# The last norm of a two-layer encoder: two of eight tiles multiplied on GpSimd, one square root for two columns, one projection block moved ahead of attention values

## The reference, cut to what matters

```python
def rms_norm(x, g):
    xf = x.astype(jnp.float32)
    y = xf * lax.rsqrt(jnp.mean(xf * xf, axis=-1, keepdims=True) + EPS)
    return (y * g.astype(jnp.float32)).astype(x.dtype)

def reference(x, ...):
    for i in range(2):
        h = rms_norm(x, mix_norm[i])
        x = x + (neighbourhood_attention(h, ...) if i == 0 else sliding_window_gqa(h, ...))
        x = x + squared_relu_mlp(rms_norm(x, mlp_norm[i]), ...)
    return rms_norm(x, final_norm)
```

## Time and profile before

| | |
|---|---|
| time, median of 3 runs (lowest, highest) | 1142.25 us (1141.94, 1142.47) |
| the profiled execution's own time | 1142.17 us |
| its span, first to last instruction | 1140.5 us |
| PE busy | 1128.4 us, 99% of the span |
| DVE, ACT, POOL busy | 633.2, 512.3, 134.6 us |
| HBM read, written | 103.84 MB, 2.67 MB |

### The profile page before, as it was taken

How to read it: one execution, slowest core, us unless ns; L and a number is a source line. 1 busy time by engine, 2 the same in 40 slices (tenths; PEclk the granted TensorE clock), 3 DMA queues, 4 the chain that set the end, 5 groups by cost and what they waited for, 6 DMA issues and landing times.

```text
span 1140.5 us, 16574 instructions
## 1 busy us (share of the span) xinstructions
PE 1128.4 (99%) x5580; PEld 943.0 (83%) x5580; DVE 633.2 (56%) x1030; ACT 512.3 (45%) x922; POOL 134.6 (12%) x243
## 2 busy tenths in 40 slices
PE   8999999999999999999999999999999999999997
PEld 6888888888888888888888888888888888888886
DVE  7787887764442234444346888866443223444334
ACT  6777777553431124333235676644443122333221
POOL 6543341330000000000001222100000000000000
PEclk9999999999999999999999999999999999999999
DMA  6222231343222322232322112122223222332222
GB/s 227 94 91 91 93 91 55 98 120 105 92 92 97 106 92 92 94 108 77 108 92 93 45 59 60 52 93 93 92 92 102 101 92 92 99 103 93 92 92 93
DMA packets 34290, 106.97 MB, mean 94 GB/s; under 512 B 5760, under 2 KB 8096, under 8 KB 34256
## 3 DMA queue, kind: packets, MB, share of 16 engines
q1 hardware_dynamic: 29344, 98.61, 25.7%
q0 software_dynamic: 4768, 7.90, 2.9%
q10 hardware_dynamic: 144, 0.02, 0.0%
HBM read 103.84 MB, written 2.67 MB: 93 GB/s over the span
## 4 chain that ended last, share of the span: by engine, by line
PE 98%; DVE 0%; DMA 0%; ACT 0%; SPq 0%; issue 0%; DVEq 0%; ACTq 0%
PE acc L427 28%; PE acc L429 28%; PE acc L428 28%; PE om_ps L565 2%; PE pt_ps L741 2%; PE om_ps L589 1%; PE om_ps L561 1%; PE s_ps L531 1%; PE pt_ps L552 1%; PE s_ps L730 1%; PE s_ps L729 1%; PE om_ps L521 1%; PE s_ps L427 1%; PE s_ps L429 1%; PE s_ps L428 1%; DMA w_raw<-in_wstream 0%
## 5 line engine op out<-in xcount | busy, mean ns | idle before, releaser
L839 ACT CAST w_hi<-w_raw 128x1024 fp32r<-128x1024 f32 x179 | 187.9, 1050 | 387.8 <-PE acc L429 382.8
L427 PE MATMUL acc<-h_hi,w_hi 128*128 128x512 f32 x792 | 315.5, 398 | 1.7 <-DVE w_lo L1140 0.9
L429 PE MATMUL acc<-h_hi,w_lo 128*128 128x512 f32 x792 | 309.1, 390 | 0.0
L428 PE MATMUL acc<-h_lo,w_hi 128*128 128x512 f32 x792 | 308.8, 390 | 0.0
L1140 DVE TENSOR_TENSOR w_lo<-w_raw,w_hi 128x1024 fp32r<-128x1024 f32 x177 | 216.6, 1224 | 143.6 <-ACT w_hi L839 143.6
L427 PE MATMUL acc<-u_hi,w_hi 128*128 128x512 f32 (+1 forms) x624 | 240.6, 386 | 0.0
L429 PE MATMUL acc<-u_hi,w_lo 128*128 128x512 f32 (+1 forms) x624 | 239.5, 384 | 0.0
L428 PE MATMUL acc<-u_lo,w_hi 128*128 128x512 f32 (+1 forms) x624 | 239.5, 384 | 0.0
L427 PEld LDWEIGHTS acc<-h_hi,w_hi 128*128 128x128 f32 x792 | 148.8, 188 | 33.0 <-issue 1.9
L429 PEld LDWEIGHTS acc<-h_hi,w_lo 128*128 128x128 f32 x792 | 148.7, 188 | 31.7
L428 PEld LDWEIGHTS acc<-h_lo,w_hi 128*128 128x128 f32 x792 | 148.9, 188 | 28.5 <-issue 0.7
(11 more groups left out here) (158 smaller groups left out, 1060.1 us busy)
## 6 DMA issues: line engine op xcount, KB each, us to landing
w_raw<-in_wstream SPq DMA_DIRECT2D x180, 512.0 KB, 3.3
bias_pairs<-rpb_reversed POOLq DMA_DIRECT2D x64, 62.0 KB, 2.4
bias_pairs<-t_shifted POOLq DMA_DIRECT2D x64, 48.0 KB, 2.5
x_res<-in_xT SPq DMA_DIRECT2D x8, 256.0 KB, 5.7
out_y<-x_res SPq DMA_DIRECT2D x8, 128.0 KB, 1.8
out_y<-x_res SPq DMA_DIRECT2D x4, 256.0 KB, 2.3
t_shifted<-vT POOLq DMA_DIRECT2D x16, 31.0 KB, 2.1
mask<-in_mask POOLq DMA_DIRECT2D x1, 64.0 KB, 5.5
```

The lines of the kernel that those rows point to most:

```text
L427: nc.tensor.matmul(dst, a[0], b[0], start=start, stop=False)
L428: nc.tensor.matmul(dst, a[0], b[1], start=False, stop=False)
L429: return nc.tensor.matmul(dst, a[1], b[0], start=False, stop=stop)
L839: nc.scalar.copy(w_hi[:, c.odd, :], w_raw[:, c.odd, :]).then_inc(w_hi_made, 1)
```

## The change

The first half of the tiles and the first three quarters of the kernel stay as they are. Four things change.

- Two of the eight tiles of the second token half, 4 and 5, are no longer multiplied by DVE. ACT multiplies them with their gain while the second half of the last group runs, PE spreads the reciprocal deviation a second time into another PSUM tile, ACT copies that to SBUF (`rstd_copy`, in the space of `o_raw`), and POOL multiplies the two tiles with it, in place. SP's third store of the second half waits for POOL's two products; its fourth waits for the sixth of DVE's.
- The two columns of the statistics lie side by side in one PSUM tile; the matmuls have a two-column operand (`pick`) of ones and zeros, which POOL fills earlier, and one activation takes both square roots.
- POOL's last work is now those two products, at the end of the program.
- Block 12 of the output projection is issued ahead of `sw_values` of unit (7, 2) instead of behind the transposition of unit (7, 3).

```diff
@@ SP @@
-            for k in range(0, KT, 2):
-                sp.wait_ge(y_made, KT + k + 2)
+            for n, k in enumerate((0, 2, 4, 6)):
+                if k == POOL_TILES[0]:
+                    sp.wait_ge(y_by_pool, 2)
+                else:
+                    sp.wait_ge(y_made, KT + min(2 * n + 2, KT - 2))
                 sp.dma_start(out[k:k + 2, :, half_tokens[1]].rearrange("k p t -> p k t"),
                              x[:, k:k + 2, half_tokens[1]]).then_inc(y_stored, 16)
@@ POOL @@
+            nc.gpsimd.memset(pick[:], 0.0).then_inc(pool_filled, 1)
+            pool.wait_ge(pool_filled, 3)
+            nc.gpsimd.memset(pick[:, 1:2], 1.0).then_inc(pool_filled, 1)
             split_weights(CH_MLP1 + 2)
+            pool.wait_ge(rstd_copied, 1)
+            for k in POOL_TILES:
+                pool.wait_ge(x_gained, k - POOL_TILES[0] + 1)
+                nc.gpsimd.tensor_tensor(x[:, k, half_tokens[1]], x[:, k, half_tokens[1]], rstd_copy, ALU.mult).then_inc(y_by_pool, 1)
@@ PE @@
+                            pe.wait_ge(pool_filled, 4)
-                                    nc.tensor.matmul(last_stats[h][b], sqsum[:, (2 * h + b) * P:(2 * h + b + 1) * P],
-                                                     ones[:, 0:1], start=True, stop=False)
+                                    nc.tensor.matmul(last_stats[h], sqsum[:, (2 * h + b) * P:(2 * h + b + 1) * P],
+                                                     pick[:, 1 - b:3 - b], start=b == 0, stop=False)
...
                     ins = nc.tensor.transpose(last_rstd[n][:, b, :], last_std[:, n, b:b + 1].to_broadcast([P, P]), ident[:])
                 ins.then_inc(last_rstd_done, 1)
+                if n == 1:
+                    for b in range(2):
+                        ins = nc.tensor.transpose(rstd_again[:, b, :], last_std[:, n, b:b + 1].to_broadcast([P, P]), ident[:])
+                    ins.then_inc(last_rstd_done, 1)
...
                     dense_part(2 * n + 1)
+                    if n == 3 and last == 8:
+                        dense_part(2 * n + 2)
                     if before or n >= 1:
                         sw_values(*sw_unit_by(p, n, -1))
...
-            early_part(CH_SWO, GR_SWO, HEADS, 12, 14)
+            early_part(CH_SWO, GR_SWO, HEADS, 13, 14)
@@ ACT @@
-                    for b in range(2):
-                        ins = nc.scalar.activation(last_std[:, n, b:b + 1], last_stats[n][b], ACT.Sqrt, bias=eps[:],
-                                                   scale=1.0 / D)
-                    ins.then_inc(std_made, 1)
+                    nc.scalar.activation(last_std[:, n, :], last_stats[n], ACT.Sqrt, bias=eps[:],
+                                         scale=1.0 / D).then_inc(std_made, 1)
+                    if n == 0:
+                        for k in POOL_TILES:
+                            nc.scalar.activation(x[:, k, half_tokens[1]], x[:, k, half_tokens[1]], ACT.Copy,
+                                                 scale=gain[:, 4 * KT + k:4 * KT + k + 1]).then_inc(x_gained, 1)
+                act.wait_ge(last_rstd_done, 3)
+                nc.scalar.copy(rstd_copy, flat(rstd_again)).then_inc(rstd_copied, 1)
@@ DVE @@
                 for k in range(KT):
-                    result(1, k)
+                    if k not in POOL_TILES:
+                        result(1, k)
```

More of the change, by code:

```diff
@@ L25 @@
 HD, HEADS, KV = 64, 16, 4
+POOL_TILES = (4, 5)
 ROWS, COLS = 8, 64
@@ L146, in encoder @@
         t5_row = vT[0:HEADS, :]
-        last_std = sb("last_std", [P, 2, 2])
+        last_std, pick = sb("last_std", [P, 2, 2]), sb("pick", [P, 3])
         sw_sink, sw_nsink = sb("sw_sink", [P, 2, 2]), sb("sw_nsink", [P, 2, 2])
@@ L194, in encoder @@
         last_rstd_done = sem("last_rstd_done")
+        x_gained, rstd_copied, y_by_pool = sem("x_gained"), sem("rstd_copied"), sem("y_by_pool")
         half_tokens = [slice(0, SEQ // 2), slice(SEQ // 2, SEQ)]
-        last_stats = [[misc_ps[:, 0, 0:1], o_ps[:, 0, 0:1]], [pt_ps[:, 0, 0:1], s_ps[:, 0, 0:1]]]
+        last_stats = [misc_ps[:, 0, 0:2], pt_ps[:, 0, 0:2]]
         last_rstd = [misc_ps[:, 2:4, :], pt_ps[:, 2:4, :]]
+        rstd_again, rstd_copy = s_ps[:, 0, 0:2 * P].rearrange("p (b q) -> p b q", b=2), o_raw[:].rearrange("p h j d -> p (h j d)")
         spare_hi, spare_lo = (t[:, 0:2, :].rearrange("p a b -> p (a b)") for t in (u_hi, u_lo))
@@ L677, in last_statistics @@
                 for b in range(2):
-                    ins = nc.tensor.matmul(last_stats[n][b], last_square[:, (2 * n + b) * P:(2 * n + b + 1) * P],
-                                           ones[:, 0:1], start=False, stop=True)
+                    ins = nc.tensor.matmul(last_stats[n], last_square[:, (2 * n + b) * P:(2 * n + b + 1) * P],
+                                           pick[:, 1 - b:3 - b], start=False, stop=b == 1)
                 ins.then_inc(stat_done, 1)
```

## The result

The changed kernel takes **1144.99 us** (median of 11 runs, 1144.69 to 1145.57) against 1142.21 us of the kernel before in the same comparison: ratio 1.0025, 95% interval 1.0016 to 1.0034, 2.78 us slower. The forecast was 1145.3 us, slower. The span of the profiled execution went from 1140.5 to 1143.2 us.

What follows compares the result with a forecast made beforehand. PE holds 98% of the chain of waits. Gain of 0.66 from the block; products end at 1136.03, 7.33 of drain and 0.2 follow, so the span ends 3.06 us later: 1145.3 us, 8-in-10 range 1142.5 to 1146.6.

Steps and rivals of the forecast that it cites:

- POOL's end: End of program: POOL's closing drain, 7.33 us of its own, lies bare behind its second product; span ends 3.06 us later.
- that other end: POOL's drain runs beside its products; all 9.71 us count from the first product, 1134.62, giving a time of 1146.3 us.
- the moved block: Around 741 us: block 12 fills PE's wait before the values of unit (7, 2); gain 0.66 us.
- the one square root: Last norm, second half: one activation for both columns moves the rest of the chain up by 0.16 us.
- The second spreading: PE spreads the deviation again from 1133.97; two transpositions take 0.43 us, four at most 0.86, to 1134.83.
- the lateness of the values: Around 741 us: with block 12 in the hole the values start at 741.71, 0.03 us late.
- Two tiles on POOL: Last norm: POOL's two products take 1.41 us; last store issued up to 0.75 us earlier, end moves only 0.16.
- its lower end: For two tiles on POOL: 0.16 us if the store pipe is full, against 0.75 if it could go faster.
- a full pipe: Last four stores, 1136.42 to 1139.55, run without a gap at DMA share 1.01; their end moves only with their start.
- A short or hidden drain: Rival, program's end: drain under 3.4 us, only the gains count, 1141.4 us, or 1140.8 with faster stores; chance 0.16.
- A part of it: Rival, program's end: 3.4 to 6.5 us of the drain is left, time 1141.5 to 1144.5 us; chance 0.05.
- POOL shut out by DVE: Rival, last norm: POOL's products wait for DVE's, ending 1.6 us later; 1146.9 us with the drain, about 1142.4 without; chance 0.03.

Runs made afterwards that it cites:

- the early drain: The changed kernel with one more drain in POOL's queue, right behind the weight chunk at 787 us: 1141.30 us, ratio 0.9992 against the kernel before.

## Why the prediction was right

**POOL's end** was the step that carried the sign, and it held in size and in order. Expected: products done at 1136.03, 7.33 of drain behind them, 0.2 to the end. Measured: 1135.65, 7.32, and 0.23 (1142.97 to 1143.2). The drain runs behind the products, as chosen, and not beside them from their start; that other end would have given 1146.3. Three runs with the drain moved, removed or bared (1141.30, 1141.31, 5.0 us more) show that it is the cause, and the run with all products on DVE (1141.24) that the moved block and the one square root cost nothing.

**What was off by tenths.** The products ended 0.38 earlier than forecast. The program reached POOL's weight chunk at 787.10, where 788.00 - 0.66 = 787.34 was expected: 0.24, of which 0.18 is a difference of the two programs' starts (at the transpositions ahead of blocks 10 and 11, 738.95 and 738.77) and the rest the moved block. The second spreading gave another 0.22: four transpositions took 0.64 (1133.11 to 1133.75) where I had put twice the 0.43 of two. The square root, the copy and the handovers took 0.08 of this back. ACT's copy took 0.37 for 0.36 and POOL's products 1.41 for 1.41. So the forecast came out 0.3 us above the measured median.

**The moved block** was forecast at 0.66 and is 0.70 in the traces of its own run and of the kernel before. Block 13 now starts 4.49 us after the transpositions ahead of blocks 10 and 11 (738.97 to 743.46), where block 12 started 4.50 after them before (738.95 to 743.45). So the lateness of the values, forecast at 0.03, does not last, and the whole block falls out. The wait is gone from the trace and no other came in its place: in that run PE's list of waits from 735 us to the end holds the two of the earlier trace rows and no third. **The square root** was forecast at 0.16 and is 0.13 in the trace: the reciprocal starts 0.33 us behind the single activation (1132.56 to 1132.89 after), a little more than the 0.28 behind the second of the two before (1133.62 to 1133.90).

**Two tiles on POOL** gain nothing, for the reason that the forecast took its lower end: the stores are a full pipe. DVE's products end 0.8 us sooner, but with the drain out of the way (1141.30) the kernel is no faster than with all eight on DVE (1141.24). DVE and POOL did not slow each other: DVE's six products took 2.44, 0.41 each, and POOL's two 1.41, as before. The Trainium skill ("SBUF — State Buffer", section "SBUF: two separate sides") has a DVE operation take the port pair that it shares with GpSimd if it runs in a 2-port mode or has two inputs in SBUF. This trace agrees as far as it goes: DVE's products, with one of the two tensors in PSUM, and POOL's ran together at their usual lengths.

**The rivals.** A short or hidden drain fell: 7.32 us. A part of it fell as well. POOL shut out by DVE fell with the durations just named. The rule of the Trainium skill ("VectorE: DVE Perf Modes", section "The DRAIN you can't avoid") that a program's closing drains take about 12 ns on every engine holds in the trace after for SP (7 ns) and not for POOL (7.32 us of its own). With the early drain and no DMA behind it POOL's last drain comes down to 0.10 us.

**What the forecast had by luck.** It took the drain over unchanged because both kernels issue the same DMAs. That was sound; the division by their number that I then tested was not, as the table shows. Had the change also removed some DMAs, I would have got the new length wrong, and with 101 of them left even its direction.

## What to carry to other kernels

Look at what an engine's queue does after its last instruction, not only at its work: an engine that ends early may have a long close that nobody sees, and a small piece of work placed last exposes it. Where GpSimd issues DMAs and must work at the end, give its queue a drain in a stretch where it is idle: here that one line brought the change, by medians, from 2.78 us above the kernel before to 0.81 below it. And before an engine is relieved at the end of a kernel, read the DMA share of the stores behind it; at a share of 1, as here, the relief ends in the pipe.

## What the runs showed of the hardware that I had not expected

In these kernels a drain of POOL costs 0.083 us for each DMA that POOL issued since the drain before, for 53, 64 and 101 of them, all landed hundreds of microseconds earlier; it costs 0.10 us when there are none. It is less per DMA for 149 and 213 (0.049 and 0.050), and 101 cost more than 149 (8.38 against 7.32 us). The counts other than 0 and 149 were each seen in one run.
